# Decode key pages scored in pairs, a second bank for turned weights, and value pages in runs of 2, 3 and 3

## The reference

```python
def diff_weights(s, bias, lam):
    logits = s.astype(jnp.float32) * ATT_SCALE + bias[None, None]
    p = jax.nn.softmax(logits, axis=-1)
    return p[:, 0] - lam * p[:, 1]
...
    s_past = jnp.einsum('bqhjd,bkhjd->bjhqk', q2, k_past.reshape(B, P, H, 2, DIFF_HEAD_DIM))
    s_new = jnp.einsum('bqhjd,bkhjd->bjhqk', q2, k_new.reshape(B, T, H, 2, DIFF_HEAD_DIM))
```

## Time and profile before

| what | value |
|---|---|
| time, median of 3 runs | 1884.76 us |
| lowest and highest | 1882.25 and 1884.78 us |
| time of the profiled execution | 1881.49 us |
| its span, first to last instruction | 1879.9 us |
| mean granted TensorE clock | 0.981 of full speed |
| PE busy, share of the span | 95% |
| DVE busy, ACT busy | 50%, 29% |
| slot 0 starts, slot 16 starts, output projection starts | 281.7, 463.9, 584.8 us |

### The profile page before, as it was taken

How to read it: one execution, slowest core, us unless ns; L and a number is a source line. 1 busy time by engine, 2 the same in 40 slices (tenths; PEclk the granted TensorE clock), 3 DMA queues, 4 the chain that set the end, 5 groups by cost and what they waited for, 6 DMA issues and landing times.

```text
span 1879.9 us, 33059 instructions
## 1 busy us (share of the span) xinstructions
PE 1789.7 (95%) x13461; PEld 1653.0 (88%) x13461; DVE 940.0 (50%) x1245; ACT 548.8 (29%) x993; POOL 91.7 (5%) x138
## 2 busy tenths in 40 slices
PE   7999998999988999998999999999999999999996
PEld 6999995665557999996789899999999999999995
DVE  6327887886665487222343853332233332233456
ACT  6202115776656266004332621110000000000133
POOL 2100001001220000001000000000000000000001
PEclk9999999999998999998999999999999999999997
DMA  5421217766794334135302411111111111111322
GB/s 175 130 68 59 66 67 226 218 190 197 256 305 176 116 113 158 68 112 178 137 25 76 161 59 51 57 47 45 45 45 45 45 45 45 45 45 39 135 75 92
DMA packets 149374, 199.06 MB, mean 106 GB/s; under 512 B 8105, under 2 KB 110715, under 8 KB 148872
## 3 DMA queue, kind: packets, MB, share of 16 engines
q1 hardware_dynamic: 134318, 133.00, 23.2%
q0 software_dynamic: 14944, 64.53, 9.7%
q10 hardware_dynamic: 2, 0.00, 0.0%
HBM read 177.19 MB, written 20.74 MB: 105 GB/s over the span
## 4 chain that ended last, share of the span: by engine, by line
PE 85%; DVE 7%; ACT 5%; issue 2%; DMA 0%; SPq 0%; POOLq 0%; POOL 0%; DVEq 0%; ACTq 0%
PE PS L1823 20%; PE PS L1824 20%; PE PS L1825 20%; PE PS L1813 8%; PE PS L2099 2%; PE PS L2075 2%; PE PS L2053 2%; PE PS L2378 2%; PE PS L2136 1%; PE PS L2399 1%; DVE WL L1550 1%; PE PS L2275 1%; PE PS L1862 1%; PE PS L2276 1%; PE PS L2277 1%
## 5 line engine op out<-in xcount | busy, mean ns | idle before, releaser
L1823 PE MATMUL PS<-XH,WH 128*128 128x352 f32 x1984 | 643.9, 325 | 2.1 <-DVE TA L1730 2.1
L1824 PE MATMUL PS<-XL,WH 128*128 128x352 f32 x1984 | 637.5, 321 | 0.0
L1825 PE MATMUL PS<-XH,WL 128*128 128x352 f32 x1984 | 637.0, 321 | 0.0
L1196 DVE CAST WH<-RAW 128x1024 fp32r<-128x1024 f32 x112 | 78.8, 704 | 633.8 <-PE PS L1825 612.0
L1823 PEld LDWEIGHTS PS<-XH,WH 128*128 128x128 f32 x1984 | 373.6, 188 | 3.2 <-DVE TA L1730 2.3
L1824 PEld LDWEIGHTS PS<-XL,WH 128*128 128x128 f32 x1984 | 374.2, 189 | 0.0
L1825 PEld LDWEIGHTS PS<-XH,WL 128*128 128x128 f32 x1984 | 373.2, 188 | 0.0
L1310 DVE SCALAR_TENSOR_TENSOR CY<-GP,DW,CY 128x1024 f32<-128x1024 f32 x124 | 158.7, 1280 | 1.0 <-DVE CY L1313 1.0
L1823 PE MATMUL PS<-HH,WH 128*128 128x352 f32 x468 | 153.1, 327 | 2.9 <-DVE Y L1769 2.9
L1824 PE MATMUL PS<-HL,WH 128*128 128x352 f32 x468 | 151.6, 324 | 0.0
L1825 PE MATMUL PS<-HH,WL 128*128 128x352 f32 x468 | 151.5, 324 | 0.0
(11 more groups left out here) (342 smaller groups left out, 2298.8 us busy)
## 6 DMA issues: line engine op xcount, KB each, us to landing
PG<-in_cache_k SPq DMA_DIRECT2D x128, 256.0 KB, 2.9
PG<-in_cache_v SPq DMA_DIRECT2D x64, 256.0 KB, 4.2
PG<-in_cache_v POOLq DMA_DIRECT2D x64, 256.0 KB, 4.3
RAW<-in_w_gate SPq DMA_DIRECT2D x22, 512.0 KB, 4.0
RAW<-in_w_up SPq DMA_DIRECT2D x22, 512.0 KB, 5.2
RAW<-in_w_in SPq DMA_DIRECT2D x20, 512.0 KB, 6.3
RAW<-in_w_out SPq DMA_DIRECT2D x16, 512.0 KB, 4.8
RAW<-in_w_xo SPq DMA_DIRECT2D x16, 512.0 KB, 4.3
```

Source lines behind the costliest of these rows:

```text
L1196: dve.tensor_copy(WH[v % 2][:, :, :], raw).then_inc(hi_done, 1)
L1823: pe.matmul(out, WH[u][:, k, :], xh[:, k, cols], start=(k == 0), stop=False)
L1824: pe.matmul(out, WH[u][:, k, :], xl[:, k, cols], start=False, stop=False)
L1825: mm = pe.matmul(out, WL[u][:, k, :], xh[:, k, cols], start=False, stop=(k == kt - 1))
```

## The change

- **Key pages in pairs.** `KTS` becomes two buffers of two pages each. `turn_keys` runs for each page as before, but the scores are made by `pair_scores` after every second page, for the two pages that were turned before: 4 matmuls with 256 moving columns in place of 8 with 128. After slot 15 one `pair_scores` stands in place of two `page_scores`. `KNEW` and the page table `PT` move to other addresses to make room for the fourth buffer.
- **A bank for the second portion of weights.** In slots whose weights belong to the value phase, `turn_weights` portion 1 goes to bank 6 and no longer waits for ACT's copy of portion 0. `turn_values(0)` moves from bank 6 to bank 5.
- **Value pages in runs.** The value phase gets a loop body of its own, `attend_values`: pages 0 and 1; `turn_new`, convolution work and both portions of `turn_weights`; pages 2, 3 and 4; further convolution work, `values` and `turn_probs`; pages 5, 6 and 7; then the last convolution work.

```diff
-        KTS = [at(f"KTS{i}", [P, 512], F32, R1 + (49152, 51200, 65536)[i]) for i in range(3)]
+        KTS_AT = (49152, 51200, 65536, R2B - R1 + 21216 + 2 * TB4)
+        KTS = [at(f"KTS{i}", [P, 2, (KTS_AT[2 * i + 1] - KTS_AT[2 * i]) // 4], F32, R1 + KTS_AT[2 * i]) for i in range(2)]
...
+        def weight_bank(h, qb, g):
+
+            return 6 if g and slot(h, qb) >= KV else 4
...
-                copy(WT[:, a:b, :].rearrange("p a t -> p (a t)"), PS[:, 4, 0:P * (b - a)]).then_inc(wt_ok, 1)
+                copy(WT[:, a:b, :].rearrange("p a t -> p (a t)"), PS[:, weight_bank(h, qb, g), 0:P * (b - a)]).then_inc(wt_ok, 1)
...
-                copy(KTS[n % 3][:, :], PS[:, 6 + n % 2, :]).then_inc(k_taken, 1)
+                copy(KTS[n // 2 % 2][:, n % 2, 0:512], PS[:, 6 + n % 2, :]).then_inc(k_taken, 1)
...
-                pe.wait_ge(wt_ok, group0(h, qb) + g)
+                bank = weight_bank(h, qb, g)
+                if bank == 4:
+                    pe.wait_ge(wt_ok, group0(h, qb) + g)
                 for k in range(a, b):
-                    x = turn(PS[:, 4, P * (k - a):P * (k - a) + P], PB[qb % 2][:, 0, P * k:P * k + P])
+                    x = turn(PS[:, bank, P * (k - a):P * (k - a) + P], PB[qb % 2][:, 0, P * k:P * k + P])
...
-            def page_scores(n):
+            def pair_scores(n):
...
-                pe.wait_ge(k_taken, n + 1)
+                pe.wait_ge(k_taken, n + 2)
...
-                    x = pe.matmul(PS[32 * h:32 * h + 32, 5, P * j4:P * j4 + P], QZB[:, own:own + 32],
-                                  KTS[n % 3][:, P * h:P * h + P], start=(n % PAGES == 0), stop=(n % PAGES == PAGES - 1),
-                                  skip_group_check=True)
+                    x = pe.matmul(PS[32 * h:32 * h + 32, 5, P * j4:P * j4 + 2 * P].rearrange("p (a t) -> p a t", a=2),
+                                  QZB[:, own:own + 32], KTS[n // 2 % 2][:, :, P * h:P * h + P],
+                                  start=(n % PAGES == 0), stop=(n % PAGES == PAGES - 2), skip_group_check=True)
...
             def key_page(n):
                 turn_keys(n)
-                if n >= 2:
-                    page_scores(n - 2)
+                if n % 2 and n >= 3:
+                    pair_scores(n - 3)
...
+                scores(h, qb)
+                if s in (KV, KV + QT):
+                    clear_values(s // QT - 2)
+                pages(0, 2)
+                if probs is not None and s % QT == 4:
+                    turn_new(probs)
+                if len(blocks) > 0:
+                    conv_block(blocks[0])
+                if len(back):
+                    conv_return(back[0])
+                    head_half(s - BACK_AT, 0, 3)
+                for g in range(len(groups(last[1]))):
+                    turn_weights(*last, g)
+                if s == KV + QT:
+                    turn_values(0)
+                pages(2, 5)
+                if len(back):
+                    conv_return(back[1])
+                    head_half(s - BACK_AT, 1, 3)
+                values(*last)
+                if probs is not None and s % QT >= 4:
+                    turn_probs(probs, s % QT - 4)
+                pages(5, 8)
+                if len(blocks) > 1:
+                    conv_block(blocks[1])
+                if len(back):
+                    conv_return(back[2])
```

More of the change, by code:

```diff
@@ L171, in hymba_step @@
         ST = [at(f"ST{i}", [P, T], F32, R2B + 21216 + TB4 * i) for i in range(2)]
-        KNEW = at("KNEW", [TS, 512], F32, R2B + 21216 + 2 * TB4)
+        KNEW = at("KNEW", [TS, 512], F32, R1 + 40960)
         VNEW = at("VNEW", [TS, 512], F32, R2B + 21216 + 2 * TB4 + 2048)
@@ L175, in hymba_step @@
         CY = at("CY", [P, CT, T], F32, R3 + 16384)
-        PT = at("PT", [P, P], I32, R2B + 21216 + 2 * TB4)[64:65, :]
+        PT = at("PT", [P, P], I32, R2B + 21216 + 2 * TB4 + 2048)[64:65, :]
         OTHER = at("OTHER", [TS, DB], F32, RC + 1824 + 352)
@@ L1417, in values_pick @@
                 dve.tensor_copy(PM[:, P * g:P * g + P].rearrange("p (n r) -> p n r", r=ROWS),
-                                PS[:, 6, :].rearrange("p (n w) -> p n w", w=32)[:, :, 0:ROWS]).then_inc(ob_out, 1)
+                                PS[:, 5 + g, :].rearrange("p (n w) -> p n w", w=32)[:, :, 0:ROWS]).then_inc(ob_out, 1)
             def natural(t):
@@ L2098, in page_scores @@
                     own = QG * g + P * b4 + 32 * h
-                    x = pe.matmul(PS[32 * h:32 * h + 32, 5, P * j4:P * j4 + P], QZB[:, own:own + 32],
-                                  KTS[n % 3][:, P * h:P * h + P], start=(n % PAGES == 0), stop=(n % PAGES == PAGES - 1),
-                                  skip_group_check=True)
-                if n % PAGES == PAGES - 1:
+                    x = pe.matmul(PS[32 * h:32 * h + 32, 5, P * j4:P * j4 + 2 * P].rearrange("p (a t) -> p a t", a=2),
+                                  QZB[:, own:own + 32], KTS[n // 2 % 2][:, :, P * h:P * h + P],
+                                  start=(n % PAGES == 0), stop=(n % PAGES == PAGES - 2), skip_group_check=True)
+                if n % PAGES == PAGES - 2:
                     x.then_inc(s_done, 1)
@@ L2153, in turn_values @@
                     pe.wait_ge(ob_out, g)
+                else:
+                    pe.wait_ge(cy_nat, BLOCKS)
                 for b in range(4):
-                    x = turn(PS[:, 6, P * b:P * b + P], OB[:, P * b:P * b + P])
+                    x = turn(PS[:, 5 + g, P * b:P * b + P], OB[:, P * b:P * b + P])
                 x.then_inc(ob_turned, 1)
@@ L2170, in conv_return @@
             def conv_return(n):
+                if n == 0:
+                    pe.wait_ge(ob_out, 1)
                 pe.wait_ge(cy_normed, 4 if n < 2 * CT and n % 2 == 0 else BLOCKS)
@@ L2246, in _, with attend_values, pages @@
                 attend(s, lambda t: key_page(8 * s + t))
-            for n in (8 * KV - 2, 8 * KV - 1):
-                page_scores(n)
+            pair_scores(8 * KV - 2)
+            def attend_values(s):
+                h, qb = ORDER[s]
+                last = ORDER[s - 1]
+                blocks, back = conv_blocks(s), conv_back(s)
+                probs = softmax_group(s)
+                def pages(a, b):
+                    for t in range(a, b):
+                        value_page(8 * (s - KV) + t)
+                scores(h, qb)
[25 more added lines that the diff above has]
+                    conv_return(back[2])
             for s in range(KV, NH * QT):
-                attend(s, lambda t: value_page(8 * (s - KV) + t))
+                attend_values(s)
             turn_weights(NH - 1, 0, 0)
```

## The result

Four runs of the changed kernel took 1861.26 to 1865.06 us, median 1863.55; four of the kernel before 1882.25 to 1884.78, median 1884.47. The ratio is 0.9895 [0.988, 0.991]: 20.9 us less. The profiled execution took 1861.26 us with a span of 1859.7, against 1881.5 and 1879.9.

A forecast was written before the change was run, and what follows sets the result against it. PE was taken to bound the kernel (85% of the span), DVE close behind in the key phase. Pairs 13.0, bank 5.6 and runs 0.7 sum to 19.3 us: 1884.8 - 19.3 = 1865.5 us, range 1858 to 1879.

The forecast's parts named there:

- The pair: Key phase: one pair costs 0.74 us for two groups' 1.06, saving 0.32, or 1.28 us per slot of 4 pairs.
- the 0.53 charged: Slots 1 to 4 and 9 to 12: no score group fills the wait between weight portions, so 0.53 us is lost, 0.75 saved.
- the 0.32 for the last pair: Slot 15: 0.32 us saved by the last pair replacing two groups, within 1.4 us for the slot.
- DVE's idle time as a cap: Key phase: DVE's idle time in a slot limits the saving kept; slots 5 to 7 keep 2.6 of 3.8 us.
- 0.2 us off slot 10: Slot 10: 0.2 us of the saving withheld for DVE, within 4.9 us kept for slots 9 to 14.
- Slot 12: Slot 12: 0.4 us of the saving withheld, since a DVE copy behind the tap releases the slot's end.
- Slots 0 and 1: Slot 0 saves nothing, as DVE's edge work releases slot 1's weights; slot 1 saves 0.5 us.
- Bank and runs: Value phase: bank saves 0.7 us in each of eight slots, 5.6 us; runs save 0.7 us for slots 20 and 23.
- A: Rival, key phase: ACT becomes the bound, the 13.0 us go and 6.3 stay, 1878.5 us; chance 0.10.
- B: Rival, key phase: strips don't overlap for wider columns, a pair costs 1.03 us and saves 0.03, 1877.5 us; chance 0.05.
- D: Rival, value phase: value pages come too late; if A holds too, nothing is left, 1884.8 us; chance with A 0.04.
- C: Rival, key slots: TensorE's clock falls after longer PE waits, up to 26.1 us lost against 19.3 won, 1891.6 us; chance 0.06.

The follow-up runs named there:

- the experiment that fills the gap: Changed kernel with the first pair of slots 1 to 4 and 9 to 12 moved behind the first weight portion: median 1859.99 us, ratio 0.9881.
- short taps: Convolution taps of slots 1 to 7 and 9 to 14 cut to 128 of 1024 columns: 1884.87 us in the kernel before, 1864.11 in the changed one.
- the added DVE work: Changed kernel with one more DVE instruction, result unused, in each of the 13 tap slots: 1871.56 us.
- bank alone: Kernel before, with only the second portion of weights in bank 6 during the value phase and turn_values(0) in bank 5: ratio 0.9985.
- runs alone: Kernel before, with the new value-phase loop body but both portions of weights still in bank 4: ratio 1.0005.
- new weights first: Changed kernel with DVE's copy of the turned new weights ahead of the convolution tap in slots 12 and 20: median 1859.45 us, ratio 0.9886.
- pairs alone: Changed kernel without the second bank and the runs of value pages, key pages still scored in pairs: median 1867.43 us, ratio 0.992.
- the version with both last edits: Changed kernel with the first pair behind the first weight portion and the new-weights copy ahead of the tap: median 1857.16 us, ratio 0.9868.

## Why the prediction was right

The forecast was 1865.5 us and 19.3 us saved; 1863.55 and 20.9 were measured. By stretch, against the spans: key phase 13.0 forecast, 13.86 measured; slots 16 to 30 6.3 forecast, 4.46 measured; 1.6 us lie before slot 0, where the two programs are the same, and belong to no term. The total is closer than its terms: slots 2 to 7 gave 6.68 us for the 4.85 forecast, and slots 0, 1, 15, 16 and 25 gave less than their share. That these nearly cancel, and that the stretches outside the change favoured the changed kernel, is luck.

**The pair.** Its price came out to the hundredth: 0.74 us. The 1.28 us per slot with one portion are 1.22, 1.27, 1.20, 1.25, 1.21 and 1.28 us in slots 5 to 8, 13 and 14. The 0.75 per slot with two portions are 0.74, 0.85, 0.75 and 0.74 in slots 3, 4, 9 and 11, and the experiment that fills the gap gives about 0.47 of the 0.53 charged. Slot 2 gave 1.40, more than either figure. In the kernel before, the first score group for a new filling of bank 5 waited there until DVE's copy had emptied the bank (line 1485), and the forecast had no term for this wait:

```profile
318.62 0.69 DVE L1485 COPY SD<-PS 128x512 f32<-128x512 f32 x1
319.43 0.19 PEld L2099 LDWEIGHTS PS<-KTS,QZB 128*32 128x32 f32 x8 [0.79 <-issue]
```

In the changed kernel the pair comes later and its gap is the usual 0.17. The 0.62 us less of waiting and the 0.75 make 1.37.

Slot 15 gave 1.11 for 1.4. In the kernel before, its last three groups stood right behind one another and took 1.29 us of loads and gaps, not 3 x 0.53, so most of the 0.32 for the last pair had nothing to come from. In the changed kernel the last two pairs take 1.60, not 2 x 0.74, since the last one waits for the copy of the last page:

```profile
447.91 0.16 PEld L2106 LDWEIGHTS PS<-KTS,QZB 128*32 128x32 f32 x8 [0.70 <-ACT KTS L738]
```

**DVE's idle time as a cap: this step failed.** "DVE's idle time in the same slot gives the most of it that can be kept" is not so. Slots 5 to 7 gave 3.69 us where the step allowed 2.6. With short taps they gave the same, so no part of the gain was held back by DVE. The 2.6 was the sum of the waits in the list, while DVE's idle time in these slots was 3.25 us; but 3.25 would have been too little as well. Idle time counts how long DVE waited for its inputs. What PE feels is whether DVE's output is late, and between the scaled weights and their turn there was slack, 0.7 us in slot 7 even with DVE at no idle time. The slack is finite: with the added DVE work, and in slot 11 with the pair moved, PE did wait for DVE.

The same rule took 0.2 us off slot 10, which gave 0.62 for 0.75. Short taps leave that slot within 0.01 us of 11.80, so DVE isn't what kept the 0.13 back. PE's first loads of key pages in the slot, before and changed, and ACT's copies in front of the second:

```profile
401.39 0.42 PEld L1813 LDWEIGHTS PS<-IDENT,PG 128*128 128x128 f32 x4 [1.35 <-issue]
390.56 1.09 ACT L738 ACTIVATE KTS<-PS 128x512 f32<-128x512 f32 x2
391.27 0.90 PEld L1818 LDWEIGHTS PS<-IDENT,PG 128*128 128x128 f32 x8 [1.43 <-issue]
```

The wait grew by 0.08 us. The profile names no releaser, but the program waits there for ACT's copy of an earlier page, and in both kernels PE goes on some 0.1 us after the first of these copies ends. ACT comes to them late because it has just worked through the exponentials of the decode scores. Most of the 0.13 is this.

**Slot 12** was forecast correctly: 0.46 us less than its share, for 0.4 forecast, held by the copy behind the tap. Slots 9 to 14 then come to 4.89 us for 4.9, though the 0.2 forecast for DVE in slot 10 was in fact 0.13, and not DVE's.

**Slots 0 and 1** gave -0.07 us for 0.5, and this can't be resolved. Their sum is 32.69, 32.58 and 32.30 us in three executions with the key pages of before (the profiled one, bank alone, runs alone) and 32.76, 32.85 and 31.78 in three that don't differ there from the changed kernel (itself, new weights first, pairs alone). The granted clock over slot 1 was between 0.74 and 0.90 in all thirteen executions.

**Bank and runs.** 6.3 us were forecast. Slots 17 to 20 gave 3.13, 21 to 23 0.17, 26 to 28 2.29: 5.6 us. What is missing from these to the 4.46 is slots 16 and 25, which grew by 0.45 and 0.72 us. In both, the granted clock was 1.00 before and 0.84 and 0.82 after. Slot 25 of the same program at full clock, from the version with both last edits, beside slot 25 of the kernel before:

```profile
508.57:516.51 7.94, 6.91 (x96) 4.85 (x97) 4.76 (x8) 3.93 (x10) 1.84 (x4) 1.00 1.01 349
```

```profile
530.83:539.62 8.79, 7.28 (x96) 4.73 (x96) 4.75 (x8) 3.96 (x10) 1.83 (x4) 1.00 0.90 303
```

At equal clock slot 25 saves 0.85 us, and the term comes to 6.5 us for 6.3. The forecast's split into 0.7 for the bank and 0.7 in all for the runs was wrong, though: the 0.7 us of a slot need both edits. And the gain that was put down to slots 20 and 23 isn't there in slot 23, which kept its 4.52 us; slot 20 gave 0.88, and slot 22 0.14.

**The rivals.** A (ACT's copies bind) asked for PE's waits to name `KTS`. PE's weight loads in slots 2 to 14 of the changed kernel:

```profile
PEld PS L1818 <- issue: 24.2, 50, 2.0
PEld PS L2106 <- issue: 8.4, 50, 0.2
...
PEld PS L2106 <- ACT KTS L738: 1.7, 2, 1.5
```

1.7 us in two waits. The one of 1.5 is in slot 8, where it was 1.65 in the kernel before. Some waits for ACT stand under `issue`, as in slot 10, but that one grew by only 0.08. The slots gave what the pair saves, so A falls; waiting for ACT's page copies costs more than before in slots 10 and 15 only, 0.08 and 0.3 us. By this the trace doesn't bear out, for this kernel, the bound that the Trainium skill names as possible (TensorEngine Tiling (Array Packing), Performance Considerations, PSUM Bottleneck). B falls by the 0.74 us of a pair, for 1.03 by its reckoning. D falls too: slot 23 took 4.52 us as before, at a DMA share of 1.01 and 382 GB/s (1.00 and 378 in the earlier trace rows), so it may well be set by its pages, but slots 17 to 20 and 26 to 28 went faster regardless. C is right in kind but not in size: the clock was below 1.00 in slots 1, 16 and 25 of the changed kernel, not in 12. In other runs it did fall in slot 12, to 0.88 and 0.92 over the slot, where PE had waited 2.89 and 3.85 us there; after waits of 2.00 and 2.67 us it stayed at 1.00. Against the shortest length seen for the same program that is 0.45 us in slot 16 (10.73 for 10.28) and 1.57 in slot 25 (9.51 for 7.94). In the tap slots shown, 7 and 10, it stayed at 1.00, with transposes closer together than before. The Trainium skill (TensorE: Matmul & The Clock Gate, Part 4: PE-mode transpose) says that transposes don't engage the full clock. The trace disagrees as far as it goes: in slot 7 transposes are 3.7 of the 5.0 us of loads at a clock of 1.00, but other matmuls stand between them.

## What to carry to other kernels

Where small matmuls in array strips alternate with full-array work, count the changes of mode, not the matmuls: one group for two saved 0.3 us here, whether it was made of 8 wide instructions or 16 narrow ones. The idle time of the engine behind the critical one is no bound on what a slot gains; compare when its output is ready with when it is used, and test it by taking the work away. That slack is used up as the lateness carries over from slot to slot, so look at several slots together. When an edit is worth a microsecond, compare the stretches of the profile that it touches: most of them repeat to 0.02 us here where whole times scatter by 2 and more. And look for a short instruction that the critical engine waits for behind a long one that nobody does; moving it was worth 1.58 us.

## What the runs showed of the hardware

The gap after a strip group is 0.20 us for 128 columns and 0.41 for 256, the gap into it 0.17 wherever PE waits for nothing else. Sixteen narrow instructions and eight wide ones cost the same, 0.75 and 0.74 us, because the gap behind shrinks by what the loads grow.

The granted clock differs between executions of one program, in the slots where PE has waited long. Slot 25 of the changed kernel's program lasted 9.51 us at 0.82 and 7.94 at 1.00, in the kernel before (with short taps, which don't reach it) 10.37 at 0.84 against 8.79 at 1.00. Slot 16 took 10.28 at 1.00 and 11.33 at 0.85 in two executions of the changed value phase. Slots 16 and 25 can so hide or feign 2.6 us of an edit, and a difference that stands in such a slot alone shows nothing.
